# Differential attention on one core: scores as three rounded passes over high and low parts instead of one float32 product

## What is computed

```python
q = rms_norm(q.reshape(bsz, seq, C_HEADS, 2, C_HEAD_DIM), q_gain) * (C_HEAD_DIM ** -0.5)
k = rms_norm(k.reshape(bsz, seq, C_HEADS, 2, C_HEAD_DIM), k_gain)
logits = jnp.einsum('bqhrd,bkhrd->bhrqk', q_blk, k).astype(jnp.float32) - slopes * dist
logits = jnp.where(dist >= 0, logits, -jnp.inf)
probs = jax.nn.softmax(logits, axis=-1)
attn = probs[:, :, 0] - lam * probs[:, :, 1]
o = jnp.einsum('bhqk,bkhe->bqhe', attn.astype(v.dtype), v)
```

## Time and profile before

| | us |
|---|---|
| median of 3 runs (lowest, highest) | 2639.75 (2637.3, 2645.99) |
| the profiled execution, its own time | 2643.91 |
| span of its records | 2642.1 |
| attention phase, from the first PE work after the norm to the last transposes | about 741 to 963 |
| PE busy over the span | 2593.2 |

### The profile page before, as it was taken

One profiled execution on the slowest core, in us unless ns is written; L12 is line 12 of the kernel. 1 busy time (PEld: TensorE's weight loads), 2 busy tenths in 40 slices (PEclk: granted clock), 3 DMA queues, 4 the chain that ended last, 5 costly groups with the idle time before them and its releaser, 6 DMA issues.

```text
span 2642.1 us, 39072 instructions
## 1 busy us (share of the span) xinstructions
PE 2593.2 (98%) x14420; PEld 2133.6 (81%) x14420; DVE 1893.2 (72%) x2723; ACT 1281.6 (49%) x2260; POOL 1325.4 (50%) x1720
## 2 busy tenths in 40 slices
PE   9999999999999999999999999999999999999999
PEld 7777778888866678888887888788887666789998
DVE  4766578997676657999854477888875776786663
ACT  4455344444355544444432254455554776455553
POOL 5543543334865455433386866533336555643333
PEclk9999999999999999999999999999999999999999
DMA  5211135554321213555332312255543221233332
GB/s 147 66 49 41 57 120 160 160 160 144 101 67 56 64 56 96 176 168 171 124 120 72 95 61 60 88 168 164 170 138 96 61 59 56 59 102 96 96 97 88
DMA packets 359671, 272.77 MB, mean 103 GB/s; under 512 B 9786, under 2 KB 346052, under 8 KB 359492
## 3 DMA queue, kind: packets, MB, share of 16 engines
q1 hardware_dynamic: 343618, 216.68, 27.7%
q10 hardware_dynamic: 15874, 53.67, 5.9%
HBM read 268.22 MB, written 2.10 MB: 102 GB/s over the span
## 4 chain that ended last, share of the span: by engine, by line
PE 79%; POOL 7%; DVE 6%; issue 5%; ACT 1%; DMA 1%; ACTq 0%; POOLq 0%; DVEq 0%; SPq 0%
PE pair L1378 8%; PE pair L1375 8%; PE pair L1379 8%; POOL w_lo L563 5%; PE ps L1340 4%; PE ps L1343 4%; PE ps L1342 4%; PE ps L2617 3%; PE ps L2619 3%; PE ps L2618 3%; PE pair L1340 3%; PE pair L1343 3%; PE pair L1342 3%; PE ps L653 3%; PE ps L655 2%
## 5 line engine op out<-in xcount | busy, mean ns | idle before, releaser
L632 POOL TENSOR_TENSOR w_lo<-w_raw,w_hi 128x256 fp32r<-128x256 f32 x512 | 482.7, 965 | 763.8 <-ACT w_hi L1457 763.8
L563 POOL TENSOR_TENSOR w_lo<-w_raw,w_hi 128x256 fp32r<-128x256 f32 x588 | 482.5, 851 | 12.3
L1375 PE MATMUL pair<-m_hi,w_hi 128*128 128x512 f32 x1008 | 395.6, 392 | 4.4 <-DVE h L1681 4.4
L1378 PE MATMUL pair<-m_lo,w_hi 128*128 128x512 f32 x1008 | 396.2, 393 | 0.0
L1379 PE MATMUL pair<-m_hi,w_lo 128*128 128x512 f32 x1008 | 395.1, 392 | 0.0
L569 POOL TENSOR_TENSOR slot_mark<-slot_mark 128x1 f32<-128x1 f32 x168 | 44.2, 263 | 507.3 <-PE ps L655 218.1
L1375 PEld LDWEIGHTS pair<-m_hi,w_hi 128*128 128x128 f32 x1008 | 190.3, 189 | 40.6 <-issue 5.0
L1379 PEld LDWEIGHTS pair<-m_hi,w_lo 128*128 128x128 f32 x1008 | 189.7, 188 | 40.9
L653 PE MATMUL ps<-x_hi,w_hi 128*128 128x512 f32 x528 | 218.3, 414 | 4.3 <-DVE x_lo L1147 2.4
L1466 ACT ACTIVATE w_hi<-w_raw 128x512 fp32r<-128x512 f32 x216 | 135.3, 628 | 178.9 <-DVE w_raw L1646 96.8
L1457 ACT ACTIVATE w_hi<-w_raw 128x512 fp32r<-128x512 f32 x256 | 157.6, 624 | 123.3 <-DMA w_raw<-in_w_mlp_dram 43.3
(11 more groups left out here) (529 smaller groups left out, 7020.3 us busy)
## 6 DMA issues: line engine op xcount, KB each, us to landing
w_raw<-in_w_mlp_dram SPq DMA_DIRECT2D x112, 512.0 KB, 5.3
w_raw<-in_mlp_w_dram SPq DMA_DIRECT2D x112, 512.0 KB, 4.9
arena<-in_ada_w_dram ACTq DMA_DIRECT2D x96, 512.0 KB, 4.4
w_raw<-in_w_in_ab_dram SPq DMA_DIRECT2D x28, 512.0 KB, 3.6
w_raw<-in_w_qkv_o_dram SPq DMA_DIRECT2D x24, 512.0 KB, 3.6
w_raw<-in_w_qkv_dram SPq DMA_DIRECT2D x24, 512.0 KB, 3.7
w_raw<-in_w_in_e_dram SPq DMA_DIRECT2D x23, 512.0 KB, 3.9
arena<-in_w_mlp_dram SPq DMA_DIRECT2D x16, 512.0 KB, 5.2
```

The costliest lines, as they stand in the source:

```text
L563: last = nc.gpsimd.tensor_tensor(w_lo[:, j, k, :], w_raw[:, j, k, :], w_hi[:, j, k, :].bitcast(F32), ALU.subtract)
L632: last = nc.gpsimd.tensor_tensor(half_slot(w_lo, n)[:, k, :], g_half(hp, c)[:, k, :], half_slot(w_hi, n)[:, k, :].bitcast(F32), ALU.subtract)
L1375: first = nc.tensor.matmul(bank[:, :], hi[:, t, :], m_hi[:, m, :], start=(t == 0), stop=False)
L1378: nc.tensor.matmul(bank[:, :], hi[:, t, :], m_lo[:, m, :], start=False, stop=False)
```

## The change

The scores of an item become three passes with F32R operands: high q by high k, high q by low k, low q by high k, each on both row halves, one after the other into the same two banks. For this q and k of each unit are split after they are normalised: ACT rounds (`normal_high`, L2872 in the new numbering), DVE subtracts (`normal_rest`, L2956) and writes the low part over the normalised value's own memory (`at_qk_lo` lies on `at_q` and `at_k`). The high parts of even units lie in a new tile `at_qk_hi`, those of odd units in `m_hi[:, 7, :]` and `m_lo[:, 7, :]`. In the loop ACT rounds q of unit u + 1 in item 0 and k in item 1, behind the copy of the transposed rows; DVE subtracts for q in item 1, behind diff, and for k in item 2, ahead of diff. PE's wait now counts three steps, the normalisation, the rounding and the subtraction.

```diff
+        at_qk_lo = nc.alloc_sbuf_tensor_at("at_qk_lo", [P, 4, T], F32R, offset=arena_start)
+        at_qk_hi = nc.alloc_sbuf_tensor_at("at_qk_hi", [P, 2, T], F32R, offset=arena_start + 4 * 22 * T)
...
+        def at_high(w, c):
+            return (m_lo if c else m_hi)[:, 7, :] if w % 2 else at_qk_hi[:, c, :]
+
+        def at_low(w, c):
+            return at_qk_lo[:, 2 * c + w % 2, :]
...
-                    pe.wait_ge(f.q_n, u + 1)
-                    pe.wait_ge(f.k_n, u + 1)
+                    pe.wait_ge(f.q_n, 3 * u + 3)
+                    pe.wait_ge(f.k_n, 3 * u + 3)
                 if g >= 3:
                     pe.wait_ge(at_kept, g - 2)
-                for r in range(2):
-                    half = slice(64 * r, 64 * r + 64)
-                    last = nc.tensor.matmul(pair[g % 3][:, r, 0:n], at_q[u % 2][half, b * P:(b + 1) * P],
-                                            at_k[u % 2][half, 0:n], start=True, stop=True)
+                passes = [(at_high(u, 0), at_high(u, 1)), (at_high(u, 0), at_low(u, 1)), (at_low(u, 0), at_high(u, 1))]
+                for step, (q, k) in enumerate(passes):
+                    for r in range(2):
+                        half = slice(64 * r, 64 * r + 64)
+                        last = nc.tensor.matmul(pair[g % 3][:, r, 0:n], q[half, b * P:(b + 1) * P], k[half, 0:n],
+                                                start=(step == 0), stop=(step == 2))
                 last.then_inc(at_z, 1)
...
+            def normal_high(w, c):
+                act.wait_ge((f.q_n, f.k_n)[c], 3 * w + 1)
+                nc.scalar.activation(at_high(w, c), (at_q, at_k)[c][w % 2], ACT.Copy).then_inc((f.q_n, f.k_n)[c], 1)
...
             full_high(act, 3, 4, at_w)
+            normal_high(0, 0)
+            normal_high(0, 1)
             full_high(act, 3, 5, at_w)
...
                                      pair[g % 3][:, 0, 0:n].rearrange("p (k t) -> p k t", t=P), ACT.Copy).then_inc(at_kept, 1)
+                if u < 7 and i < 2:
+                    normal_high(u + 1, i)
                 if i == (2 if u == 7 else 1) and u:
                     o_high(u - 1)
...
+            def normal_rest(w, c):
+                v.wait_ge((f.q_n, f.k_n)[c], 3 * w + 2)
+                nc.vector.tensor_tensor(at_low(w, c), (at_q, at_k)[c][w % 2], at_high(w, c).bitcast(F32), ALU.subtract
+                                        ).then_inc((f.q_n, f.k_n)[c], 1)
...
             full_low(v, 3, 4, at_w)
+            normal_rest(0, 0)
+            normal_rest(0, 1)
             f.rooted(v, "q", 1)
...
                 nc.vector.tensor_scalar(p0, p0, at_col(g, "inv")[:, 0:1], None, ALU.mult).then_inc(*at_share("p0"))
+                if i == 2 and u < 7:
+                    normal_rest(u + 1, 1)
                 v.wait_ge(*at_share.at(g, "p0"))
                 nc.vector.scalar_tensor_tensor(out=p0, in0=p1, scalar=at_col(g, "lam")[:, 1:2], in1=p0, op0=ALU.mult,
                                                op1=ALU.add).then_inc(*at_share("diff"))
+                if i == 1 and u < 7:
+                    normal_rest(u + 1, 0)
                 for n_out in out_ends(u, i, 0):
                     add_half(v, "out_o", 0, n_out, 1.0)
                 maxima(g + 2)
```

## The result

The changed kernel takes 2655.26 us (median of 6 runs, 2653.64 to 2657.4), the kernel before 2642.53 beside it: ratio 1.005, interval 1.0039 to 1.006, 12.7 us slower. The forecast was 2644.1 with a range of 2637 to 2654. 2.8 us of that miss is the kernel before, which ran 2642.53 here instead of 2639.75; the difference itself was forecast as +4.3.

A forecast was written before the change was run, and what follows sets the result against it. PE was taken to bound the kernel, busy for 2593 of 2642.1 us. The terms -1.9 + 0.7 + 3.5 + 2.0 gave +4.3 us on the median of 2639.75, so 2644.1 us, range 2637 to 2654.

The forecast's parts named there:

- The passes: Steady part: three rounded passes, row halves side by side, replace float32 scores; wide items gain, narrow ones lose: -1.9 us.
- B: Rival: rounded passes on the two row halves take turns, six instead of three; +19.7 us, 2659 us; chance 0.14.
- C: Rival: only the narrow 128-key passes are dear, 0.47 us more instead of 0.08; together +7.4 us; chance 0.14.
- The splits in the steady part: Later units: k's subtraction delays the next unit's first scores by 0.15 us in five units; +0.7 us, bounds 0 and 4.
- D: Rival: k's subtraction is late in all seven units and meets POOL, 4.6 us; together +8.2 us; chance 0.09.
- The splits in the opening: Unit 0: first scores wait for both subtractions on DVE, delaying the chain to the first diff; +3.5 us.
- The half clock behind the pause: Opening: PE's pause of some 4.0 us brings clock 0.50 on scores and projection; +2.0 us, bounds 0 and 3.0.
- The range's scatter of 3 us: Whole kernel: allowance for scatter between runs, 3 us, included in the range for the median.
- that pause of 3.90 us: PE's pause before 391.72 us, followed by clock 0.50 that lost 3.0 us; used to price the opening's pause.
- The rule weighed there: Scores: packed tiles would cost 1.3 times their ideal, wide items gain nothing, the sum about 3.5 us higher.
- case A: The forecast itself: pairs of passes run side by side, whole kernel between +1 and +7 us; chance 0.58.

The follow-up runs named there:

- split_only: The changed kernel with all splits and their waits kept but the scores back in float32 from unsplit operands; 2649.58 us, ratio 1.0029 to the kernel before.
- filled: The changed kernel with 18 extra 512-column passes ahead of PE's wait for the splits of unit 0; 2644.68 us, ratio 1.0009 to the kernel before.
- after_padded: The changed kernel with eight already reached waits of PE per item, 128 more instructions; 2646.7 us, ratio 1.002 to the kernel before.
- before_padded: The kernel before with eight already reached waits of PE per item, 128 more instructions; 2649.06 us, ratio 1.0023 to the kernel before.
- unit0_float32: The changed kernel with the scores of unit 0 left in float32 and no splits in the opening; 2643.46 us, ratio 1.0 to the kernel before.
- before_again: The kernel before, unchanged, run once more as its own control; 2642.93 us, ratio 0.9994.
- delay26: The kernel before with 26 extra 512-column passes on PE in the attention phase; 2650.33 us, ratio 1.0027 to the kernel before.

## Why the prediction was wrong

**Right, by its steps.**
- The passes, -1.9 forecast: -2.3 measured (`split_only` to the changed kernel). The halves run side by side, the pace of a pair is 0.22 to 0.23, 0.17 and 0.12 to 0.13 us against the 0.227, 0.174 and 0.120 assumed, the 128-key group 0.48 against 0.50. Rivals B and C fall.
- The splits in the steady part, +0.7: +0.5 measured (`split_only`). k's subtraction ran at 0.68 to 0.69 us, and the 512-key scores came 0.1 us late in five units, where 0.15 was forecast. D falls.
- The splits in the opening, +3.5: 3.5 measured (`filled`), and that exactness is luck. The subtractions took 1.13 us each instead of 0.9, so the first scores came 4.6 us late instead of 3.95 (19.22 us behind the start of the phase in `filled`, 14.60 before), and PE paused for 4.65 us instead of about 4.0. Against it the forecast gave the three groups 2.86 - 0.36 = 2.5 us, but 0.66 of the 2.86 is the wait for `rooted`, which is gone once the scores are late; they took 1.77 (757.55 to 759.32). The two errors, +0.7 and -0.7, cancel.
- The half clock behind the pause, +2.0: 2.5 measured (`filled`). It set in at 759.7, 1.1 us before the pause ended, so five sixths of the stretch fell on work, not two thirds.
- So the attention phase: +4.3 forecast, +4.1 in the profile, +4.3 in `after_padded`.

**Wrong.** The step that failed is the sum. It took the attention phase's terms for the whole: "-1.9 + 0.7 + 3.5 + 2.0 = +4.3 us". All that lies behind the phase was put at nothing, without a reason given, and no rival had a loss there. What the runs showed in its place: the extra instructions shift the fetches of PE's stream onto the weight loads of the second and the third MLP, and PE waits longer there and loses clock. The range's scatter of 3 us did not cover it. `before_padded` prices that term: +6.1 us (3.4 to 8.5) for 128 more instructions in PE's stream. The changed kernel against the kernel before was +12.7, +6.9, +9.3, +12.1 and +7.1 us by medians in its five comparisons, so with 4.1 for the attention phase the term was between 2.8 and 8.6 us there. The result fell on its upper end; three of the four repeated medians (2650.57, 2652.18 and 2650.04) lie inside the stated range, so that the number left the range was in part the draw. That the term was missing was not. Each step counted the instructions of the change by their time on an engine, and none by their place in the stream. In the trace of before this could have been seen: fetches of 16 KB at nearly regular distances, a burst of loads at the second MLP that the nearest fetch missed by 11 us, half a packet, and the same burst at the first MLP with a fetch upon it. The prediction used that pause of 3.90 us for the price of a pause and did not ask what had made it.

**The rule weighed there.** By the Trainium skill, "TensorE: Matmul & The Clock Gate", section "Measured speedup vs the span model", four row tiles reach 3.07 times instead of 4. Two row halves here show no such loss: a pair at 512 columns takes 0.22 to 0.23 us, a single full pass 0.227. The forecast called 3.5 us more "still inside case A"; 4.3 + 3.5 is 7.8, which is over that case's +7 and only inside the range. By the same page of the Trainium skill, section "Back-to-back issue gap", a 512-column matmul in a stream takes 131 ns; no pass of these runs came near it, the full ones take 0.227 us.

**Open.** How one fetch makes a load of 512 KB land 2 to 3.6 us later wasn't looked into. I know only that the issue on SP takes 1.02 to 1.71 us instead of 0.58 at the second MLP, and that a fetch 0.9 us ahead of the issue does no harm there. That the fetch itself delays the load, and not something else that comes with that place in the stream, rests on how closely the two go together; no run moves one fetch alone. A pause of 2.07 us near 1631, on POOL, was followed by half clock in nine of the seventeen traces, `after_padded` and `unit0_float32` among them, and cost 1.5 to 1.9 us where it did; what decides that is not known.

## What to carry to other kernels

Count the instructions that a change adds on an engine as well as their time: their number moves every later instruction fetch against the loads, and where PE hangs on a load burst that was worth as much here as all the rest of the change. If a late phase slows down that the change doesn't touch, look for a fetch in the DMA view at its longest pause, and pad the stream by half a packet of idle waits before explaining it by the change. Ask of a long pause in the old trace, too, what made it. And a split that lies ahead of PE's first need is paid in full, and once more in clock: leaving the first unit as it was took back 6 us here.

## What the hardware showed that was not expected

- The first load of L492 ahead of the MLP pauses, three MLPs in seventeen traces: with a 16 KB fetch for PE's stream between 0.6 us ahead of its issue and 0.2 us behind it, it landed after 6.9 to 9.7 us in 28 cases and after 5.2 and 5.3 in two. With the fetch elsewhere it took 5.0 to 5.4 us in 20 cases and 5.8 in one, where the fetch came 0.45 us behind the issue.
- PE's pauses of 2.29 to 4.47 us at the two later MLPs were followed by 3.4 or 6.8 us at clock 0.50, thirteen of thirteen; of the 21 pauses of 0.37 to 1.93 us two were (`split_only`, 1.93, and `filled`, 1.81). At the first MLP it is less sharp: a pause of 2.75 us (`before_again`) and one of 2.18 (`delay26`) were not followed by half clock, one of 2.01 (`filled`) was. And in `delay26` 3.4 us at clock 0.50 (from 1716.9) followed a pause of 1.80 us ahead of the third MLP, which the table doesn't hold.
- Already reached waits on PE are nearly free: 128 more in the attention phase left it at 28.40 and 193.00 us.
- Rounded passes on two row halves start 0 to 39 ns apart in the changed kernel and overlap fully, as float32 ones do.
